# Both feed-forwards of a conditioned decoder block in one structure: seven block products in place of eight, modulation columns through a ring

## Reference

```
cond = silu(c);  mod = cond @ w_ada + b_ada          # 9 vectors of 1024
sh1, sc1, gt1, sh2, sc2, gt2, sh3, sc3, gt3 = split(mod, 9)
h = rms_norm(x, g_ffn1) * (1 + sc1) + sh1
x = x + 0.5 * gt1 * ((silu(h @ w1_a) * (h @ w3_a)) @ w2_a)
h = rms_norm(x, g_mix) * (1 + sc2) + sh2
x = x + gt2 * hybrid_mixer(h, ...)                   # first projection of it: "u"
h = rms_norm(x, g_ffn2) * (1 + sc3) + sh3
x = x + 0.5 * gt3 * ((silu(h @ w1_b) * (h @ w3_b)) @ w2_b)
return rms_norm(x)
```

## Time and profile before

| | us |
|---|---|
| three runs | 2349.25, 2349.53, 2350.23 (median 2349.53) |
| profiled execution, its own time | 2349.49 |
| its span | 2347.9 |
| PE busy | 2257.4 (96%) |
| POOL / DVE / ACT busy | 1203.8 / 1087.9 / 419.6 |
| first feed-forward on PE, first to last product | 58.40 to 813.7 |
| second feed-forward on PE | from 1641.6, last down tile at 2327.0 |
| mean granted clock of PE | 0.982 |

### The profile page before, as it was taken

One profiled execution on the slowest core, in us unless ns is written; L12 is line 12 of the kernel. 1 busy time (PEld: TensorE's weight loads), 2 busy tenths in 40 slices (PEclk: granted clock), 3 DMA queues, 4 the chain that ended last, 5 costly groups with the idle time before them and its releaser, 6 DMA issues.

```text
span 2347.9 us, 28051 instructions
## 1 busy us (share of the span) xinstructions
PE 2257.4 (96%) x10130; PEld 1854.9 (79%) x10130; DVE 1087.9 (46%) x1391; ACT 419.6 (18%) x569; POOL 1203.8 (51%) x876
## 2 busy tenths in 40 slices
PE   5899999999999899999999989999999999999997
PEld 4788788878888778888888877887788888888886
DVE  6654223431111589648392845344843342424256
ACT  3411000100001241010000021011621222222222
POOL 3344444444445534444444465554676666767571
PEclk8899999999999999999999999999999999999998
DMA  7335114331112143223222143421012121111111
GB/s 287 108 118 168 36 63 141 103 101 39 54 36 56 43 153 95 75 83 90 81 76 85 55 144 124 152 81 51 21 55 63 45 64 45 63 43 57 35 53 72
DMA packets 246654, 194.50 MB, mean 83 GB/s; under 512 B 21492, under 2 KB 226432, under 8 KB 245440
## 3 DMA queue, kind: packets, MB, share of 16 engines
q1 hardware_dynamic: 222944, 154.52, 21.6%
q10 hardware_dynamic: 23648, 39.20, 5.2%
HBM read 167.34 MB, written 25.17 MB: 82 GB/s over the span
## 4 chain that ended last, share of the span: by engine, by line
PE 90%; DVE 5%; POOL 2%; ACT 1%; issue 1%; DMA 0%; SPq 0%; DVEq 0%; POOLq 0%; ACTq 0%
PE unit_a L714 22%; PE unit_b L714 22%; PE unit_c L714 7%; PE unit_d L714 7%; PE unit_b L992 5%; PE unit_d L876 5%; PE unit_d L992 4%; PE unit_c L876 4%; PE unit_c L992 3%; PE unit_a L992 3%; PE unit_d L1110 1%; DVE rstd L1541 1%; PE unit_c L837 1%; PE unit_c L1095 1%; PE unit_d L1085 1%
## 5 line engine op out<-in xcount | busy, mean ns | idle before, releaser
L612 POOL TENSOR_TENSOR w_high<-raw,ones 128x512 fp32r<-128x512 f32 x272 | 370.5, 1362 | 846.3 <-PE unit_a L714 279.8
L614 POOL TENSOR_TENSOR w_low<-raw,w_high 128x512 fp32r<-128x512 f32 x272 | 377.0, 1386 | 21.4
L714 PE MATMUL unit_a<-h_high,w_high 128*128 128x512 f32 x736 | 230.2, 394 | 5.5 <-POOL w_low L614 4.7
L714 PE MATMUL unit_a<-h_low,w_high 128*128 128x512 f32 x736 | 227.8, 391 | 0.0
L714 PE MATMUL unit_a<-h_high,w_low 128*128 128x512 f32 x736 | 227.5, 390 | 0.0
L714 PE MATMUL unit_b<-h_high,w_high 128*128 128x512 f32 x736 | 227.1, 390 | 0.0
L714 PE MATMUL unit_b<-h_high,w_low 128*128 128x512 f32 x736 | 226.6, 389 | 0.0
L714 PE MATMUL unit_b<-h_low,w_high 128*128 128x512 f32 x736 | 226.6, 389 | 0.0
L655 POOL TENSOR_TENSOR w_low<-raw,w_high 128x512 fp32r<-128x512 f32 x100 | 135.2, 1352 | 88.3 <-ACT w_high L1419 81.0
L714 PEld LDWEIGHTS unit_a<-h_high,w_high 128*128 128x128 f32 x736 | 137.6, 189 | 34.5 <-POOL w_low L614 5.1
L714 PEld LDWEIGHTS unit_a<-h_low,w_high 128*128 128x128 f32 x736 | 139.1, 189 | 29.3
(11 more groups left out here) (367 smaller groups left out, 4357.3 us busy)
## 6 DMA issues: line engine op xcount, KB each, us to landing
raw<-in_w_b SPq DMA_DIRECT2D x66, 512.0 KB, 3.9
raw<-in_w_a SPq DMA_DIRECT2D x60, 512.0 KB, 4.1
raw<-in_w_in SPq DMA_DIRECT2D x44, 512.0 KB, 3.8
ada_raw<-in_w_ada SPq DMA_DIRECT2D x8, 2048.0 KB, 7.9
ada_raw<-in_w_ada SPq DMA_DIRECT2D x8, 1536.0 KB, 6.9
ada_first<-in_w_ada SPq DMA_DIRECT2D x8, 1024.0 KB, 14.4
sg_kept<-s ACTq DMA_DIRECT2D x16, 512.0 KB, 2.6
s<-sg_kept ACTq DMA_DIRECT2D x16, 512.0 KB, 3.3
```

What stands on the lines that cost most here:

```text
L612: pool.tensor_tensor(high, raw[:, r, rows, :], one, ALU.mult).then_inc(high_split, 1)
L614: pool.tensor_tensor(w_low[:, r % 2, rows, :], raw[:, r, rows, :], high.bitcast(F32), ALU.subtract).then_inc(slab_split, 1)
L714: last = pe.matmul(unit[u][:, t], w, x[:, k, t], start=(k == 0 and part == 0), stop=(k == kts - 1 and part == 2))
```

## The change

`ffn1` gets the structure of `ffn2`; one function `ffn` on each engine now writes both. In both, ACT makes the high part of the second whole tile and of all down operands, and `first_down` moves behind the second matrix of chunk 1. The 56 modulation columns become 14 blocks of four. A block's weights come as eight pieces of 128x512 (256 KB each) into a ring of four buffers; DVE sums them into PSUM (the upper bank of unit_b, `bank(0, 3)`), ACT copies the sum to `ada_sum`, PE multiplies by ones into `bank(0, 2)`, DVE adds to `mod`. Blocks 0 and 1 are made in chunk 1's first two matrices, three blocks in the down product of each of chunks 1 to 4. At the end of `ffn1` the last four output tiles, not two, are made in halves, in units a to d.

```diff
-CHUNKS = ((0, 8), (8, 8), (16, 6))
...
+BLOCKS = (NMOD - 2 * KD) // 4
+RING_ADA = 4
+BLOCKS_DOWN = 3
...
-        ada_raw = sb("ada_raw", [P, KD, 4 * P], rA)
...
+        def ada_sums():
+
+            return bank(0, 3)
...
+            def ada_four(p, b, half):
+
+                for n in range(4):
+                    sp.wait_ge(ada_used, p + n - (RING_ADA - 1))
+                    sp.dma_start(ada_ring[n][:, :], ada_blocks[:, 4 * half + n, b, :]).then_inc(ada_piece[n], 16)
...
+                def chunk(here, ada_before, last):
+
+                    for n in (2, 3):
+                        for e in range(2):
+                            load_matrix(here, n, e)
+                    load_down(here)
+                    if last:
+                        return
+                    after = Chunk(here.c + 1)
+                    for n in range(2):
+                        for e in range(2):
+                            load_matrix(after, n, e)
+                            if ada_before:
+                                more_ada(here, 1 + 2 * n + e)
+                    if ada_before:
+                        more_ada(here, 5)
...
+            def last_four_down(f, here):
+
+                for half in range(2):
+                    t = slice(HALF * half, HALF * half + HALF)
+                    for e in range(4):
...
+                            if half == 1 and e == 0 and k == 3:
+                                statistics(1, 0)
...
+            def ada_tiles(b):
+
+                pe.wait_ge(ada_copied, b + 1)
+                if not (isinstance(b, int) and b == 0):
+                    pe.wait_ge(mod_added, b)
+                for t in range(4):
+                    last = pe.matmul(bank(0, 2)[:, t:t + 1], ada_sum[:, t * P:(t + 1) * P], ones[:, 0:1],
+                                     start=True, stop=True)
+                last.then_inc(mod_full, 1)
...
+            def chunk_down(f, here, with_ada):
+                first_tiles_down(f, here)
+                for m in range(2, KD):
+                    tile_down(f, here, m)
+                    if with_ada and m % 2 == 1:
+                        ada_tiles(here.block0 + m // 2 - 1)
+
+            def ffn(f):
+                with_ada = f.n == 0
+                whole_tiles(f)
                 here = Chunk(1)
...
+                for n in range(2):
+                    matrix(f, here, n)
+                if with_ada:
+                    ada_tiles(1)
+                first_down(f)
+                for n in (2, 3):
+                    matrix(f, here, n)
+                chunk_down(f, here, with_ada)
...
+            def ada_copy(b):
+
+                act.wait_ge(ada_used, KD * b + KD)
+                if not (isinstance(b, int) and b == 0):
+                    act.wait_ge(mod_full, b)
+                act.activation(ada_sum[:, :], ada_sums(), ACT.Copy).then_inc(ada_copied, 1)
...
+                def down(here, ada, residual_tile=None):
+
+                    for m in range(4):
+                        down_high(here, m)
+                        pair_high(here, 3, m)
...
+                    for m in range(4, KD):
+                        down_high(here, m)
+                        if ada and m == 5:
+                            ada_copy(here.block0)
...
+                    if ada:
+                        ada_copy(here.block0 + 1)
+                        ada_copy(here.block0 + 2)
...
+                if with_ada:
+                    ada_pieces(0, 0, KD, (unit_free[B_], ffn_at(f).unit[B_] + 1))
+                sum_low("t4", 4)
+                whole_product(1)
```

More of the change, by code:

```diff
@@ L617, in _ @@
+            ffn(first_ffn)
             split(0, True)
@@ L684, in _ @@
-            for n in range(1, 4):
-                matrix(here, n)
-            down(here)
-            with pool.Fori(2, PAIRED + 1) as c:
-                here = Chunk(c)
-                for n in range(4):
-                    matrix(here, n)
-                down(here)
+            ffn(second_ffn)
         @block.tensor
@@ L745, in _ @@
                 last.then_inc(setup_full, 1)
-            def ada_tiles(w, count, u):
-                for t in range(count):
-                    last = pe.matmul(unit[u][:, t:t + 1], w[:, t * P:(t + 1) * P], ones[:, 0:1], start=True, stop=True)
-                last.then_inc(ada_full, 1)
             take(A_, 1)
@@ new lines, in matrix @@
+            def matrix(f, here, n):
+                o, w, pair = here.op[n], n % 2, here.pair[n // 2]
+                done = 14 * pair + 5 * w
+                units = ffn_at(f).unit
+                uses = here.uses_up if n == 1 else 5 if n == 3 and here.first else None
+                if n % 2 == 1:
+                    if uses is not None:
+                        take(C_, units[C_] + uses)
+                    if n == 3:
+                        pe.wait_ge(f.evacuated, 14 * pair)
+                elif n == 0 and here.first:
@@ L1233, in down_squares @@
                     square_end(n, e, 0)
-            for n in range(3):
-                up("ffn1", n)
-            own.then(load_sqrt())
-            act.wait_ge(slab_used, at["ffn1.down2"].slab)
-            with nc.allow_non_contiguous_dma(reason="rows of 256 bytes"):
-                for part, c in enumerate(("c_re", "c_im")):
-                    act.dma_start(c_rows[:, part, :, :].rearrange("h k (g p) -> h (k g) p", g=2),
-                                  a[c][0].rearrange("g h p -> h g p")).then_inc(c_loaded, 16)
@@ L1244, in _, with first_squares @@
+            def first_squares(m):
+                if m == 0:
+                    own.then(load_sqrt())
+                for half in range(2):
+                    act.wait_ge(x_final, 2 * m + half + 1)
+                    square(m, half, ACC[1] + 2 * m + half - 1)
+            ffn(first_ffn, first_squares)
+            for e in range(4):
+                square_four(e, 0)
             norm(1, at["norm1"].h)
@@ L1576, in first_mod, with norm @@
                 dve.wait_ge(mod_done, part + 1)
-            def norm(n, h0, end=None):
+            def norm(n, h0, end=None, sums=None):
                 def scaled(step):
@@ L2071, in _ @@
-            here = Chunk(PAIRED)
-            for n in range(4):
-                matrix(here, n)
+            ffn(second_ffn, gate[1][:, :])
             clear_sums(3)
-            down(None, gate[1][:, :], 3, used=operand_used, first=here.down_op)
+            down(None, gate[1][:, :], 3, used=second_ffn.operand_used, first=LAST.down_op)
             dve.wait_ge(root_done, 7)
```

1065 lines of the change are left out of this document (588 added, 477 removed).

## The result

The changed kernel takes 2271.83 us (median of 4 runs, 2271.38 to 2273.88), against 2349.45 us for the kernel before in the same comparison. The ratio is 0.9672, 95% interval 0.9659 to 0.9686. A second comparison on another chip gave 2272.18 us and 0.9672 (0.9659 to 0.9685). The forecast was 2282.0: the gain is 77.6 us where 67.5 were forecast. The profiled execution took 2271.38 us, its span 2269.6. That of the second comparison took 2272.18 us.

The account below looks back on a forecast made before the run. PE, busy 96% of the span, was taken as the bound; -63.0 us through the first feed-forward and behind "u", and -4.5 in the second, sum to -67.5, so 2349.5 becomes 2282.0 us, range 2271 to 2304.

Parts of the forecast that it names:

- 240 matmuls: First feed-forward: 2928 matmuls in place of 3168, each 0.2267 us, 663.7 us in all.
- Chunk boundaries: First feed-forward: DVE's last sums and low parts run beside POOL; five boundaries at 0.4 us, +2.0 us.
- Start of the block products: Matrix 0: PE's fourth product just fits, the fifth waits behind DVE and ACT; +1.7 us, between 0 and 8.
- End of matrix 1: PE waits for block 1's copy behind DVE's last two pieces, +8.1 us; slow matmuls after the gap, +1.8.
- From PE's last product to "u": End of the first feed-forward: PE's gap before u's first product falls from 7.3 us to 3.0.
- the term of 1.7 for the statistics: End of the first feed-forward: the first half's statistics cost 1.7 us in PE's stream, as before.
- +2 given back behind "u": Behind u's start: four second-half tiles bring DVE and ACT more squares and sums, PE needs their statistics; 2 us lost.
- The second feed-forward: Start waits -3.5 us by ACT's high parts, first_down behind matrix 1 +1.0, five boundaries -2.0; together -4.5.
- DVE in the down product: Pieces of 0.75 to 0.8 us, 4.5 us of DVE per 5.44 us tile; fits by 2.5 us.
- rivals 3: Down products: slow pieces or ACT's queue make four modulation chunks lose 4 to 8 us each; 2298 to 2314, chance 0.18.
- Rival 4: Down products: sums to PSUM stretched beside POOL make DVE the bound; 2374 us, slower than before, chance 0.05.
- SP's queue at no cost: Down products: weight loads queued behind pieces are issued by 25 us and needed 20 us later; cost nothing.

Follow-up runs that it names:

- experiment 2's second run: Changed kernel, but in the second feed-forward POOL makes the high parts of the second whole tile's four operands and the first down products' four: 2278.80 us.
- the run with three moves: Changed kernel with block 1's last two pieces earlier, its modulation sum and gate earlier, and ACT's first u copy between Exp and Sin: 2271.51 us, ratio 0.9663.

## Why the prediction was right, and where it was off

- *PE bounds the kernel, and what counts is 240 matmuls.* Right: 54.4 of the 68.4 us up to "u" are these, and the rest is old waits less new ones, and no run takes the matmuls alone. 2928 x 0.2267 = 663.7, with the slow start at 2.4 (102.64 - 56.68 less 192 x 0.2267; forecast 2.5) and the modulation at 0.94 a block.
- *Chunk boundaries, 2.0 forecast.* Measured 0: 122.50 us are content alone. "I take 0.4, between 0 and 0.8" kept half of a loss that went whole; in the second feed-forward the run with POOL's high parts brings the 0.8 back.
- *Start of the block products, 1.7.* From matrix 0's start to the end of matrix 1, 142.58 (147.50 - 4.92), are 39.9 us for 39.0 of products: 0.9.
- *End of matrix 1, 8.1 + 1.8.* The wait was where and why the forecast said: the copy ends at 147.45, PE's products behind it begin at 147.50, and moving the two pieces took it away. It was 4.9, and what it drags behind was larger than I had it: from 142.58 to the second down tile 11.6 us for 3.7 of content, 8.0 in all. I sized it from the gating in the second feed-forward and added each of DVE's late parts, while the trace has these partly side by side: the last piece ends at 146.82 and the copy 0.63 later.
- *From PE's last product to "u", 3.0.* Measured 4.3. The step missed that PE takes `unit_a` and `unit_b` together, so that the second residual, behind the first tile's square and sum (1.8 us at that place), is on the path. The run that frees the unit first shows it: the wait fell by 1.8.
- *Together* 663.7 + 2.4 + 13.2 + 0 + 0.9 + 8.0 + 1.7 + 4.3 = 694.2, measured 694.3, forecast 697.7. That it closes to 0.1 is partly luck: the term of 1.7 for the statistics was not measured, and the same kernel's other profile has 695.4.
- *The start, 0.* It was 1.7 earlier in the profiled run, but the same instructions began between 56.7 and 58.7 us in the runs here, in the changed kernel's other profile at 58.12. No effect of the change is shown.
- *+2 given back behind "u".* Not shown. The 2.6 of the table agree with it by luck: the changed kernel's other profile gave back nothing (820.46 for 820.49), and alike programs took 820.3 to 823.6. PE's stop at the third slab was 4.7 us before and 3.5 after, and this slab's first 48 matmuls took 13.69 us. The releaser there changes from run to run (ACT's copy with 2.3 and 3.5 us, POOL's low part with 2.1 and 4.7, in kernels alike up to there).
- *The second feed-forward, -4.5.* This is the step that failed in size: -10.3. Term by term: ACT's high parts of the second whole tile were priced at 3.5 and are worth 3.7. Those of `first_down` had no price and are worth 2.4. The place of `first_down` was priced at +1.0, and the difference between experiment 2's second run and the kernel before is 1.0. The boundaries were priced at half of their 0.8, 2.0 in all, and all of it went, 4.0. And at the end, which had no price, 1.3 more went with the wait for `y_gain`. Together -3.7 - 2.4 + 1.0 - 4.0 - 1.3 = -10.4. I counted what POOL is spared; at a boundary what counts is what DVE is spared beside it (1.47 us for 3.47 above), since PE waits for that.
- *DVE in the down product.* Pieces of 0.75 to 0.76 us, right; the slack is 5.6 us where the forecast had 2.5. The rivals 3 and 4 fell: no lag at a chunk. Rival 4's statement that the kernel ends slower than before where a piece takes over about 1.5 us was too low a point: with 1.5 us of DVE for each piece of the down products it takes 2312.5 us, 37 below the kernel before, and the 16 us that rival 4 adds for chunk 1, which that run leaves as it is, would not make them up. The Trainium skill, in Perfetto Trace Analysis, "Optimizing Scalar/DVE Operations", gives DVE an access overhead of about 60 ns on SBUF and 125 ns on PSUM. The difference of 65 ns is not borne out: 748 ns with one operand in PSUM, 752 with both in SBUF, at 512 columns.
- *SP's queue at no cost.* Right: no wait of PE for a weight's load, though the pieces' own loads held DVE up, by 1.4 us at most in the chunk that I read.

## What to carry to other kernels

Cost a stall at the engine that waits, and then ask what the clock does behind it: here stops of 3.5 to 5 us cost 6 to 12, the stop included. Before a wait is removed, look how far ahead of PE the next chain of the busy engine ends; here DVE's lead over PE was 5 us a hundred microseconds later, and a move at "u" that brought PE forward by 4.4 us turned it into a stop of 3.5. And what moving work off an engine is worth is read from the engine that the bound waits for: 40 high parts taken off POOL, which was not the bound, were worth 5.3 us by what DVE got faster beside it. Work added to an engine with idle time is free up to its slack and dear behind it (48 instructions 1 us, 96 instructions 40).

## What the runs showed of the hardware that was not expected

- The changed kernel's window behind its stop at the third slab (columns as above):

```profile
786.40:800.00 13.60, 13.60 (x49) 11.02 (x50) 12.15 (x41) 1.02 (x1) 6.27 (x5) 0.80 0.68 190
```

  A stop of nearly the same length was followed by very different stretches at the lower of the two levels of PE's clock (1.2 and 2.4 GHz): behind 3.5 us at 786 in the changed kernel the clock was 0.80 over 13.6 us, 2.7 us lost; behind 3.5 us at 884 in the run with three moves it was 0.57 over 20 us, 8.6 lost. PE's work behind the two stops differs: products of 512 columns at 786, and small ones of 128 columns until 898 at 884. One run of that kernel of five came out 7 us faster, at a mean granted clock of 0.984 for 0.982 in the others, which would be such a stretch missing; this is only argued. What decides the length was not tried.
- A DVE instruction of 512 columns with one operand in PSUM stayed within 745 to 758 ns in all 98 sums of the changed kernel and in the 96 extra ones, while one with both in SBUF went from 752 to 1708 ns beside POOL.
